# One pass for two norms behind the experts, regrouped modulation, and a second expert held in side buffers

## The reference

```python
    for e in range(N_EXPERTS):                      # 32 experts
        he = jax.nn.silu(t @ w_gate[e]) * (t @ w_up[e])
        y = y + combine[:, e:e + 1] * (he @ w_down[e])
...
    x = x + g2 * y.reshape(b, n, d)
...
    return rms_norm(x, norm_final)                  # end of the first block
...
def rms_norm(x, gain):
    xf = x.astype(jnp.float32)
    y = xf * lax.rsqrt(jnp.mean(xf * xf, axis=-1, keepdims=True) + EPS)
    return (y * gain.astype(jnp.float32)).astype(x.dtype)
...
def modulate(h, shift, scale):
    return h * (1.0 + scale) + shift
```

## Time and profile before

| | us |
|---|---|
| median of 3 runs | 2224.56 |
| lowest and highest | 2224.03, 2225.19 |
| the profiled execution | 2226.48 |
| its span in the trace | 2224.5 |
| experts, first to last product of PE | 259.85 to 728.63 |
| end of experts to layer 0's second pair | 728.63 to 775.07 |
| mean granted TensorE clock | 0.959 |

### The profile page before, as it was taken

How to read it: one execution, slowest core, us unless ns; L and a number is a source line. 1 busy time by engine, 2 the same in 40 slices (tenths; PEclk the granted TensorE clock), 3 DMA queues, 4 the chain that set the end, 5 groups by cost and what they waited for, 6 DMA issues and landing times.

```text
span 2224.5 us, 39741 instructions
## 1 busy us (share of the span) xinstructions
PE 1998.6 (90%) x17230; PEld 1698.4 (76%) x17230; DVE 784.0 (35%) x1397; ACT 679.8 (31%) x1202; POOL 34.5 (2%) x53
## 2 busy tenths in 40 slices
PE   6999867776766899999999999998699999999999
PEld 4788544444443688999977799996489998889999
DVE  1123311101110123545434554543654442235454
ACT  3011200000000324434323344433344443334343
POOL 0000000000000000000000000000000000000000
PEclk9999898899899899999999999999899999999999
DMA  9555799999999825755652565554275466334543
GB/s 389 195 224 224 287 426 428 428 427 428 428 427 427 330 96 204 276 186 185 241 227 89 224 265 189 213 212 192 74 285 208 165 244 253 114 114 150 178 149 130
DMA packets 41003, 552.21 MB, mean 248 GB/s; under 512 B 4545, under 2 KB 4929, under 8 KB 5057
## 3 DMA queue, kind: packets, MB, share of 16 engines
q1 hardware_dynamic: 33984, 449.98, 51.3%
q0 software_dynamic: 6912, 100.67, 11.0%
HBM read 549.58 MB, written 1.05 MB: 248 GB/s over the span
## 4 chain that ended last, share of the span: by engine, by line
PE 74%; DMA 18%; DVE 3%; ACT 3%; issue 1%; SPq 0%; DVEq 0%
PE bank L407 39%; DMA ring<-in_moe 17%; PE bank L394 10%; PE bank L401 5%; PE bank L464 4%; PE bank L676 3%; PE bank L386 2%; PE bank L449 1%; PE bank L441 1%; PE bank L859 1%; PE bank L476 1%; DMA ring<-in_ada_head 1%; PE bank L775 1%; ACT work L1199 1%; PE bank L794 0%
## 5 line engine op out<-in xcount | busy, mean ns | idle before, releaser
L407 PE MATMUL bank<-xsq_parts,ring_parts 128*128 128x256 f32 x1408 | 399.7, 284 | 0.0
L407 PEld LDWEIGHTS bank<-xsq_parts,ring_parts 128*128 128x128 f32 x1408 | 271.6, 193 | 0.0
L394 PE MATMUL bank<-hT,ring 128*128 128x256 f32 x1024 | 235.7, 388 | 3.0 <-DVE mod L1509 1.8
L676 PE MATMUL bank<-ring,xsq 128*32 128x256 f32 x2048 | 145.6, 433 | 100.0 <-DMA ring<-in_moe 99.1
L394 PEld LDWEIGHTS bank<-hT,ring 128*128 128x128 f32 x1024 | 195.0, 193 | 37.2 <-issue 7.7
L1004 ACT CAST mixT_parts<-ring 128x1024 fp32r<-128x1024 f32 (+1 forms) x152 | 151.7, 1003 | 191.8 <-PE bank L407 191.8
L407 PE MATMUL bank<-xsq_parts,mixT_parts 128*128 128x256 f32 x704 | 201.8, 287 | 3.0 <-DVE hT_parts L1393 2.8
L407 PE MATMUL bank<-hT_parts,mixT_parts 128*128 128x256 f32 x704 | 200.4, 285 | 0.0
L676 PEld LDWEIGHTS bank<-ring,xsq 128*32 128x32 f32 x2048 | 67.0, 121 | 173.9 <-DMA ring<-in_moe 127.7
L407 PE MATMUL bank<-hT_parts,xn_parts 128*128 128x256 f32 x704 | 199.2, 283 | 0.0
L407 PE MATMUL bank<-xsq_parts,xn_parts 128*128 128x256 f32 x704 | 199.2, 283 | 0.0
(11 more groups left out here) (314 smaller groups left out, 3506.4 us busy)
## 6 DMA issues: line engine op xcount, KB each, us to landing
ring<-in_moe SPq DMA_DIRECT2D x96, 2048.0 KB, 12.5
ada_ring<-in_ada POOLq DMA_DIRECT2D x48, 2048.0 KB, 12.2
ring<-in_gu SPq DMA_DIRECT2D x44, 2048.0 KB, 8.1
ring<-in_down SPq DMA_DIRECT2D x32, 1408.0 KB, 6.2
ring<-in_pair SPq DMA_DIRECT2D x24, 1536.0 KB, 6.6
ring<-in_na SPq DMA_DIRECT2D x12, 2048.0 KB, 9.6
ring<-in_out SPq DMA_DIRECT2D x10, 2048.0 KB, 8.2
ring<-in_ada_head SPq DMA_DIRECT2D x3, 2048.0 KB, 16.4
```

The source lines that it names most:

```text
L394: m = mm(dst, w[:, k, lo:lo + P], h[:, k, :], start=k == 0, stop=k == KT - 1)
L407: m = mm(dst, w[a], x[b], start=start and (a, b) == (0, 0), stop=stop and a == 1)
L676: m = mm(bank[0][CAP * q:CAP * (q + 1), 0:T], xg[:, 4 * c + k, h * CAP:(h + 1) * CAP], w[:, k, q * T:(q + 1) * T], start=(c, k) == (0, 0), ...
```

## The change

Four things are changed.

First, expert 1's three chunks leave the ring (`in_moe` has 93 chunks in place of 96) and are an input of their own, `in_moe_side`. POOL loads them into the `ada_ring` as soon as modulation chunks 0, 1 and 2 are used, where chunks 3, 4 and 5 were loaded. Expert 1 reads them there (`expert_chunk`, `r` is None).

Second, the modulation of layer 0 is regrouped. Chunk 3 (which completes the scale) goes to the upper two thirds of `work` as soon as the neighbourhood attention is done with it; its rows (group 1, one chunk now) are made in the last pack, ahead of the last down product. Chunks 6 to 8 stay group 2, but chunk 6's rows are made behind the norm's sums and those of 7 and 8 behind the first pair. Chunks 4 and 5 (the gate) are a new group 3, made around the last pair; chunks 9 to 11 become group 4. SP issues chunks 6 and 7, between the loads of the first and second pair; POOL issues 8, 4, 5, 9 and so on, from the last expert chunk's use.

Third, the final norm and layer 0's norm share one pass. `norm_twice` multiplies each tile of squares by ones and by `norm_sq` (the square of the final norm's gain, made once by POOL in the place of the DFT's matrix). From the first sum ACT gets ln, exp(-1x) and exp(-0.5x); DVE multiplies the second sum by the first's inverse, ACT takes ln and exp(-0.5x) of that, and DVE multiplies the two factors. DVE then writes the input of layer 0's shift with one operation a tile, and the normed `xT` behind that.

Fourth, the layer loops run for all layers without the switch for a part of them.

```diff
-        with eng.Fori(0, E) as e:
-            expert(e)
+        expert(0, 0)
+        expert(1, None)
+        with eng.Fori(2, E) as e:
+            expert(e, e - 1)
...
+def chunks_of(g):
+    return ((0, 1, 2), (3,), (6, 7, 8), (4, 5))[g] if g < 4 else tuple(range(GROUP * (g - 1), GROUP * g))
+def group_of(i, part):
+    return (0, 1, 2, 4)[part] if i == 0 else 4 * i + part + 1
...
+def ada_place(m):
+    return m if m < 3 else SPARE if m == 3 else m + 1 if 6 <= m < 9 else m + 6 if m < 6 else m + 3
...
+SIDE = GROUP
+SPARE = 2 * GROUP
...
+    return flat(work)[:, 4 * 2 * T:] if at == SPARE else ada_ring[ada_slot(at)][:, :]
...
+        elif name == "pair_0":
+            load(0, 0)
+            for m in (6, 7):
+                sp.wait_ge(ada_used, ada_place(m) - 2)
+                sp.dma_start(ada_buffer(ada_place(m)), ins["ada2"][m]).then_inc(late_landed[ada_place(m) - SPARE], 16)
+            steps(sp, 1, count, load)
...
-    for m in range(12 * LAYERS):
-        if m == 0:
+    def chunk(at, src, landed_in):
+        if at >= 3:
+            pool.wait_ge(ada_used, at - 2)
+        pool.dma_start(ada_buffer(at), src).then_inc(landed_in, 16)
...
+    chunk(2, ins["ada2"][2], ada_landed[ada_slot(2)])
+    pool.wait_ge(na["o_done"], NA_PAIRS)
+    pool.dma_start(ada_buffer(SPARE), ins["ada2"][GROUP]).then_inc(late_landed[0], 16)
+    for c in range(3):
+        chunk(SIDE + c, ins["moe_side"][c], ada_landed[ada_slot(SIDE + c)])
+    pool.wait_ge(dft_pe, 1)
+    nc.gpsimd.tensor_tensor(norm_sq, *[vc("normf").unsqueeze(2).broadcast_to([P, KT, P])] * 2, ALU.mult).then_inc(norm_sq_ready, 1)
+    wait_used(pool, FIRST["moe"] + 3 * (E - 1) - 1)
+    for m in (8, 4, 5, *range(9, 12 * LAYERS)):
+        chunk(ada_place(m), ins["ada2"][m], ada_landed[ada_slot(ada_place(m))])
...
+    def norm_twice():
+        pe.wait_ge(norm_sq_ready, 1)
+        for k in range(KT):
+            pe.wait_ge(sq_ready, KT * 3 + k + 1)
+            a = mm(bank[3][:, 0:T], cst("ones"), xsq[:, k, :], start=k == 0, stop=k == KT - 1)
+            b = mm(bank[2][:, 0:T], norm_sq[:, k, :], xsq[:, k, :], start=k == 0, stop=k == KT - 1)
+        a.then_inc(ssq_done, 1)
+        b.then_inc(ssq_done, 1)
...
-        for c in range(GROUP):
-            m = GROUP * g + c
-            pe.wait_ge(ada_landed[ada_slot(m)], 16 * (m // 3 + 1))
-            four_tiles(group_bank(place, c), c2_wide, ada_ring[ada_slot(m)][:, :].rearrange("p (k n) -> p k n", k=KT)).then_inc(ada_used, 1)
+        for c, m in enumerate(chunks_of(g)):
+            if not lo <= c < hi:
+                continue
+            at = ada_place(m)
+            wait_place(pe, at)
+            four_tiles(group_bank(place, c), c2_wide, ada_buffer(at).rearrange("p (k n) -> p k n", k=KT)).then_inc(ada_used, 1)
...
+        if r is None:
+            wait_place(pe, SIDE + c)
+            return ada_buffer(SIDE + c)
+        wait_chunk(pe, n0 + c, r)
+        return slot(n0 + c)[:, :]
...
+            r = (0, None)[h] if first else e - 1
...
+            if last and h == PACK - 1:
+                group_rows(1, "final")
...
-        moe_branches(pe, expert, packed, turn_comb)
-        group_rows(1, "final")
-        norm(3)
+    moe_branches(pe, expert, packed, turn_comb, lambda: group_rows(1, "final"))
+    norm_twice()
...
-        pe.wait_ge(mods_taken, 4 * i + 2)
-        group_rows(4 * i + 2, "attn")
+        pe.wait_ge(mods_taken, group_of(i, 2))
+        group_rows(group_of(i, 2), "attn", 0, 1 if i == 0 else GROUP)
...
+            if i == 0:
+                group_rows(group_of(i, 2), "attn", 1)
+            group_columns(group_of(i, 2), "attn")
+            pe.wait_ge(mods_taken, group_of(i, 2) + 1)
+            if i == 0:
+                steps(pe, 1, PAIRS - 1, pair)
+                group_rows(3, "step")
+                pair(PAIRS - 1, 0)
+                group_columns(3, "step")
+                pe.wait_ge(mods_taken, 4)
...
-                wait_used(act, n0 + 2, e)
+            if last and h == PACK - 1:
+                group_out(1, "final")
...
-        norm(3, xT, (x_done, KT, 1), xT, lambda k: vc("normf", k, 1), lambda k: cst("zero"), lambda: group_out(1, "final"))
+    for k in range(KT):
+        act.wait_ge(x_done, KT + k + 1)
+        A(xsq[:, k, :], xT[:, k, :], ACT.Square).then_inc(sq_ready, 1)
+    act.wait_ge(ssq_done, 5)
+    A(qn[:, 0:T], bank[3][:, 0:T], ACT.Ln, scale=1.0 / D, bias=cst("eps")).then_inc(ln_ms, 1)
+    act.wait_ge(ln_ms, 4)
+    A(qn[:, T:2 * T], qn[:, 0:T], ACT.Exp, scale=-1.0).then_inc(ms_ready, 1)
+    A(rinv[:, :], qn[:, 0:T], ACT.Exp, scale=-0.5).then_inc(rinv_ready, 1)
+    act.wait_ge(ms_two, 1)
+    A(u_two, u_two, ACT.Ln, scale=1.0 / D, bias=cst("eps")).then_inc(ln_ms, 1)
+    act.wait_ge(ln_ms, 5)
+    A(r_two, u_two, ACT.Exp, scale=-0.5).then_inc(rinv_ready, 1)
+    for k in range(KT):
+        act.wait_ge(xn_ready, KT * 3 + k + 1)
+        A(hT[:, k, :], xn[:, k, :], ACT.Identity, bias=mod[:, k:k + 1]).then_inc(h_ready, 1)
...
-        norm(4 + 2 * i, xT, ready, hT, gcol(0), scol(mod, 0))
-        group_out(4 * i + 2, "attn")
+            norm(4 + 2 * i, xT, (x_done, KT * (1 + 2 * i), 1), hT, gcol(0), scol(mod, 0))
...
+            if i == 0:
+                group_out(group_of(i, 2), "attn")
+                steps(act, 1, PAIRS - 1, pair)
+                group_out(3, "step")
+                pair(PAIRS - 1, 0)
...
+        chunks = chunks_of(g)
+        i, lo, n = chunks[0] // 12, 4 * (chunks[0] % 12), 4 * len(chunks)
-        V.tensor_tensor(mod[:, lo:lo + 4 * GROUP], group_bank(place, GROUP), vc("b_ada2", MODS * i + lo, 4 * GROUP),
+        V.tensor_tensor(mod[:, lo:lo + n], group_bank(place, GROUP)[:, 0:n], vc("b_ada2", MODS * i + lo, n),
...
-        wait_used(dve, FIRST["moe"] + 3 * E - 1)
+    wait_used(dve, FIRST["moe"] + 3 * (E - 1) - 1)
-        normalise(3)
+    dve.wait_ge(mods_ready, 3)
+    then(V.tensor_tensor(gain[:, 1, :], gain[:, 0, :], vc("normf"), ALU.mult), "mods")
+    dve.wait_ge(ms_ready, 1)
+    V.tensor_tensor(u_two, qn[:, T:2 * T], bank[2][:, 0:T], ALU.mult).then_inc(ms_two, 1)
+    dve.wait_ge(rinv_ready, 5)
+    then(V.tensor_tensor(rr, rinv[:, :], r_two, ALU.mult), "mods")
+    for k in range(KT):
+        V.scalar_tensor_tensor(xn[:, k, :], xT[:, k, :], gain[:, 1, k:k + 1], rr, ALU.mult, ALU.mult).then_inc(xn_ready, 1)
+    for k in range(KT):
+        m = V.scalar_tensor_tensor(xT[:, k, :], xT[:, k, :], vc("normf", k, 1), rinv[:, :], ALU.mult, ALU.mult)
+    then(m, "mods")
...
+            if i == 0:
+                steps(dve, 1, PAIRS - 1, pair)
+                pair(PAIRS - 1, 0)
+                take_mods(3, "step")
...
+o["moe_side"] = o["moe"][3:6]
+o["moe"] = np.concatenate([o["moe"][:3], o["moe"][6:]])
```

638 lines of the change are left out of this document (323 added, 315 removed).

## The result

The changed kernel takes 2204.77 us (median of 4 runs, 2203.16 to 2212.56) against 2224.3 us (4 runs, 2220.37 to 2225.19) on the same chip: a ratio of 0.9926 [0.9913, 0.9939]. The forecast was 2208.6. The medians are 19.5 us apart, the ratio is worth 16.5. The profiled execution is the longest of its four: 2212.56 us, span 2210.5, which is 14.0 less than the profiled one of before. Measured again beside the later experiments, the same kernel came to 2210.43 us and a ratio of 0.9939 [0.9923, 0.9954].

What follows compares the result with a forecast made beforehand. Transfers bound the experts, a chain of short steps the stretch behind them, PE the pairs. Terms -9.6 - 11.4 + 5.0 = -16.0, from the median 2224.56 to 2208.6 us; range 2201 to 2217.

Steps and rivals of the forecast that it cites:

- term 1: Experts: three fewer ring chunks save 14.7 us of transfer, less 4.0 to 5.6 lost at the refills; taken as -9.6 us.
- term 2: From T, the end of the experts' spreading, to the second pair's projection: 35.0 us against 46.4, so -11.4 us.
- the first dry spell: Experts' ring: the queue runs dry at about 280 while PE does expert 1, a loss of 4.0 to 5.6 us.
- From the next chunk on two are queued again and the rate is as before: Experts' ring after the first refills: no further loss, as PE has 6.4 us of waiting a pack to give.
- PE's first instruction behind the branch comes 1.95 us late today; I keep that: PE behind the experts: the delay after the branch stays 1.95 us in the changed kernel.
- the sums: Behind the experts: 32 passes on PE take 10.7 us, half of them at either clock level.
- the chain: From the end of the norm's sums to the first projection: small ACT and DVE steps taking 3.8 us, today 1.9.
- PE stays warm: Rival: PE at full clock throughout, sums 7.2 us, second projection 1.7 less; -21.2 us, 2203.4, chance 0.14.
- rival with a low clock and a second gap: Behind the experts: sums take 14.2 us, plus another 1.95 us instruction gap; -10.6 us, 2214.0, chance 0.15.
- Term 3, the last pairs: Layer 0's last pairs: two chunks of rows, their columns and a DVE wait add 5.0 us on a full PE.
- POOL's multiplication: Before the experts: 2.2 us long, barely overlapping DVE's routing, taken as 0; rival that it stops routing +2.2, chance 0.09.
- The queue of SP: Chunks 6 and 7, queued ahead of the second pair's weights, delay neither the last expert chunk nor those weights.

Runs made afterwards that it cites:

- no_side: The changed kernel with expert 1 back in the ring (96 chunks) and modulation chunks 6, 7 and 8 loaded early in its place: 2216.26 us, ratio 0.9978.
- after: The changed kernel as first measured and profiled, against the kernel before the change: 2204.77 us, ratio 0.9926.
- after_again: The changed kernel measured and profiled once more, with nothing altered: 2210.43 us, ratio 0.9939.
- long_else: The kernel before the change, with two experts written out ahead of the loop in the branch not taken: 2226.49 us, ratio 1.001.
- short_else: The changed kernel with the branch that isn't taken emptied of its experts on all engines: 2199.44 us, ratio 0.9904.
- hold_loads: The changed kernel with chunks 6 to 8 issued only after chunk 3's modulation, all their rows behind the first pair: 2213.05 us, ratio 0.9959.
- late_if: The changed kernel with PE's last expert pack moved behind the jump, under an If of its own: 2199.38 us, ratio 0.9896.
- late_again: late_if measured and profiled once more, with nothing altered: 2201.47 us, ratio 0.9907.
- one_sum: late_if with seven of the eight tiles left out of the second norm sum: 2197.53 us, ratio 0.9882.

## Why the prediction was right, and where it was not

The time and the sign came out, and every large mechanism was there. The sum of the profile was -16.0 and came to -14.0, and that it came so near is in part luck: term 1 fell short by 1.3 and term 2 by 4.9, but the experts began 2.4 earlier, which isn't the change's, and the second projection ran 1.7 faster. The median hit is luck in part too: the same kernel's two medians, 2204.77 and 2210.43, lie on either side of the 2208.6.

- **Term 1, the experts: right in mechanism, near in size.** Forecast -9.6; the profiles give -8.3 and, for the same kernel again, 457.4 - 468.8 = -11.4; no_side against after gives -8.7 to -11.6 in the ratios and, to T and with equal first products, -8.3 to -11.7. Of the -8.3 of before to after, 1.3 is the last down product at full clock (1.93 for 3.18), which no term had. Of its steps, the refilled buffer was to be reached at 280.0 to 281.6 and was reached at 276.97: 2.4 because the experts began earlier, most of the rest because expert 1 took 276.97 - 265.99 = 11.0, below the 11.4 to 13.0. The seventh chunk was to wait until 291 to 293 and was taken at 286.94, also because its load took 7.8 us and not 9.1. The 9.1 of the earlier trace rows is a load with two more issued behind it; I had taken it for a load alone. So the first dry spell cost 2.4, not 4.0 to 5.6. "From the next chunk on two are queued again and the rate is as before" is the sentence that failed: in after and after_again the queue ran dry again 28 us later (302 and 339 GB/s in 296 to 312, where before it was 428), with PE at the low clock. In after the two make 6.2, above what was taken, by another way: 14.7 - 6.2 = 8.5.
- **Term 2, from T to the second pair: the step "PE's first instruction behind the branch comes 1.95 us late today; I keep that" failed.** It came 5.95 late. The prediction listed the writing-out of two experts in the diff and costed only what they do, and they are never executed; long_else and short_else show that their mere presence is the price. Forecast 35.0, measured 39.95: the gap +4.0; the columns +0.4, at low clock; the sums 9.1 (724.75 to 733.89) for 10.7, -1.6; the chain 4.1 for 3.8, +0.3; the first projection at 8.83 for 7.17, +1.7; the rest of the pair as forecast. What the profile gained is 6.5, not 11.4.
- **The clock.** I took half of the sums' passes at either level; it was about a third: two passes take 1.06 at 727.45 and 0.59 from 728.98 on, and ten of the 32 stand before that. That the first projection would also be hit, and the second at full clock in its place, I had only as the second half of the rival "PE stays warm". The two together are even: +1.7 and -1.7. Of the rival with a low clock and a second gap, half came: the gap was longer, the low clock was not.
- **Term 3, the last pairs: +5.0, measured 3.2 + 1.7 = +4.9**, the rest of the span with the second pair's projection (8.86 to 7.17) taken out. All of it stands ahead of layer 0's last suffix sum; what follows takes 1342.1 us in both. No wait for chunks 10 and 11, which were hidden as argued.
- **POOL's multiplication: 0, right.** It took 1.90 for the 2.2 estimated and was over 1.25 us before DVE's routing. Since they never met, no run here shows what they would do to each other.
- **The queue of SP: right.** PE didn't wait for the last expert chunk (the down product at 714.37 follows the rows at once) nor for the second pair's weights, and hold_loads, without chunks 6 and 7 in that place, is 1.8 us slower to the second pair.
- **The median.** I took it 1.9 below the profiled execution, as before. The profiled execution of after was 7.8 above the median of its runs. That, not a step, is why the median fell 19.5 us and the profile 14.0; why that execution was long is open.

Open: what sets the spread of one kernel's runs. It goes with the mean clock (after_again: 2203.39 us at 0.963, 2214.58 at 0.953). Between profiles of different kernels up to 9 us lie in the layers, where nothing is changed: 1335.0 us behind layer 0's last suffix sum in short_else, 1343.8 in after_again. The two pairs of profiles of one kernel differ there by 1.8 us (after, after_again) and by nothing (late_if, late_again), so that the spread of one kernel lies there too is likely, not shown. Differences of 2 to 3 us in the medians, as of late_if against one_sum or short_else, can't be told from it.

## What to carry to other kernels

Code in a branch that isn't taken can have a price where the engine jumps over it, so put such a jump where the engine waits for something else, not on a chain of short steps. A load moved out of a transfer-bound ring is worth its transfer only if it goes where the DMA engines are idle, and less what the ring's shallow lead loses while the engine works elsewhere. When a profile shows idle time that waits for nothing, ask what it depends on before carrying its length over to the new kernel.

## What was not expected of the hardware

- PE's jump over code that isn't executed: no gap with no experts in it, 1.95 + 1.94 us with one loop body, 5.05 to 5.95 us (5.22 + 1.38 in long_else) with two experts more, and not more with four (5.42 and 5.20). Moved ahead of a stretch that is short of loads it is as long (5.50 us in late_if, 5.06 in late_again, 5.37 in one_sum), and about half of it is hidden there: to T one_sum took 457.0 and short_else, which has no gap, 454.3, both without a second dry spell.
- In a stretch bound by transfers PE was at 0.50 of its clock from 292 to 308 us, busy 14.65 of 16 us, right behind 12 us at 0.99 in which it was busy 7.47. In the profiles of before and late_again the stretch from 296 to 312 is at 0.89 and 1.00. Where it was low, the ring ran dry (four profiles of seven); where it wasn't, it didn't (three).
- The cost of the low clock moved rather than vanished: in nine of twelve profiles, of two equal projections 13.5 to 20 us apart one took 8.8 to 8.9 us and the other 7.1 to 7.2.
